# Two-layer attention and expert kernel: the second attention's query rank in three rounded products, the key rotation behind the remainders, the residual's scale behind VectorE's rotation

## What is computed

```python
kv_a = x @ w_kv_a                                # 1024 -> 256 + 64
c_kv = rmsnorm(kv_a[..., :256], kv_norm_g)
k_rope = rope(kv_a[..., 256:], cos, sin)         # the keys' rotated part, shared by the heads
kv = c_kv @ w_kv_b                               # 8 heads x (128 key + 128 value)
q = rmsnorm(x @ w_q_a, q_norm_g) @ w_q_b         # 1024 -> 384 -> 8 heads x (128 + 64)
q_rope = rope(q[..., 128:], cos, sin)
logits = q_nope . k_nope + q_rope . k_rope       # chunk-causal mask, softmax
h = (softmax(logits) @ v) @ w_o
x = layernorm(ALPHA * x + h)
# experts: router, top 2 of 32 experts in one group, silu(t @ gate) * (t @ up) @ down, weighted sum
```

## Time and profile before

| | us |
|---|---|
| median of 3 runs | 702.27 (700.65 to 704.05) |
| the profiled execution, its own time | 701.2 |
| its span in the trace | 699.4 |
| TensorE matrix products busy | 669.3 (96%) |
| VectorE, ScalarE, GpSimd busy | 321.0, 214.8, 127.9 |
| share of the chain that ended last: TensorE, transfers, SyncE's issue, VectorE | 69%, 11%, 9%, 6% |
| granted TensorE clock over the span, of full speed | 0.993 |

### The profile page before, as it was taken

The page is one execution under the profiler, slowest core; times in us unless marked ns, Lnnn a source line. Parts: engine busy times, 40 slices in busy tenths (PEclk is TensorE's granted clock), DMA queues, the critical chain, the costliest instruction groups (busy, mean ns, idle before and its releaser), DMA issues.

```text
span 699.4 us, 9824 instructions
## 1 busy us (share of the span) xinstructions
PE 669.3 (96%) x3682; PEld 383.6 (55%) x3684; DVE 321.0 (46%) x657; ACT 214.8 (31%) x420; POOL 127.9 (18%) x149
## 2 busy tenths in 40 slices
PE   9999999999999999999989798999999999999993
PEld 6969878654333433445546776866534334343551
DVE  4768755744243242232274846574424323323226
ACT  4668661531111121121146136353111211111112
POOL 0404110062010100100029570006201001010000
PEclk9999999999999999999999999999999999999998
DMA  9990049899999999999996009479999999999992
GB/s 331 364 378 3 0 176 423 343 357 391 422 419 423 421 420 422 420 421 420 415 414 255 0 8 407 196 299 369 387 421 423 420 421 421 421 420 421 421 408 97
DMA packets 42829, 237.73 MB, mean 340 GB/s; under 512 B 3920, under 2 KB 4096, under 8 KB 18720
## 3 DMA queue, kind: packets, MB, share of 16 engines
q1 hardware_dynamic: 41776, 235.36, 82.9%
q10 hardware_dynamic: 576, 1.05, 0.4%
q0 software_dynamic: 432, 0.70, 0.3%
HBM read 236.04 MB, written 1.05 MB: 339 GB/s over the span
## 4 chain that ended last, share of the span: by engine, by line
PE 69%; DMA 11%; SPq 9%; DVE 6%; ACT 2%; issue 2%; POOL 0%; DVEq 0%; POOLq 0%; ACTq 0%
PE psum L595 66%; DMA ring<-in_moe_w_up 8%; SPq L477 6%; DMA ring<-in_diff_w_qkv 3%; SPq L482 2%; PE psum L1078 1%; DVE work L442 1%; DVE ln_stats L1694 1%; SPq L462 1%; PE psum L970 1%; PE psum L918 1%; SPq L464 1%; ACT scratch L1298 0%; ACT x_res L1493 0%; PE psum L701 0%
## 5 line engine op out<-in xcount | busy, mean ns | idle before, releaser
L595 PE MATMUL psum<-ring,work 128*64 128x512 f32 (+2 forms) x1360 | 229.7, 489 | 2.1 <-POOL work L2265 1.3
L595 PEld LDWEIGHTS psum<-ring,work 128*64 128x64 f32 (+1 forms) x1360 | 99.5, 138 | 130.7 <-issue 105.6
L595 PE MATMUL psum<-ring,scratch 128*64 128x512 f32 x512 | 116.9, 598 | 0.9 <-ACT scratch L1545 0.9
L2167 DVE TENSOR_TENSOR scratch<-psum,scratch 128x256 f32<-128x256 f32 x32 | 13.6, 425 | 180.1 <-ACT scratch L1541 180.1
L2247 POOL COPY work<-work 128x512 f32 x60 | 36.7, 616 | 289.4 <-PE psum L595 285.8
L1534 ACT ACTIVATE x_T_rounded<-psum,small 128x512 fp32r<-128x512 f32 x64 | 43.6, 687 | 109.5 <-DVE scratch_rounded L2148 90.9
L1541 ACT ACTIVATE scratch<-psum 128x256 f32<-128x256 f32 x32 | 12.3, 384 | 203.0 <-PE psum L595 203.0
L595 PEld LDWEIGHTS psum<-ring,scratch 128*64 128x64 f32 x512 | 33.9, 136 | 67.9 <-issue 65.0
L595 PE MATMUL psum<-x_T_rounded,scratch_rounded 128*128 128x512 f32 x144 | 62.9, 437 | 0.9 <-issue 0.8
L595 PE MATMUL psum<-ring_rounded 128*128 128x256 f32 (+1 forms) x214 | 61.6, 309 | 0.0
L595 PE MATMUL psum<-ring_rounded,x_T_rounded 128*128 128x512 f32 x192 | 60.8, 398 | 0.0
(11 more groups left out here) (270 smaller groups left out, 829.3 us busy)
## 6 DMA issues: line engine op xcount, KB each, us to landing
ring<-in_moe_w_up SPq DMA_DIRECT2D x64, 1024.0 KB, 19.9
ring<-in_moe_w_gate SPq DMA_DIRECT2D x60, 1024.0 KB, 16.9
ring<-in_moe_w_down SPq DMA_DIRECT2D x60, 1024.0 KB, 20.0
ring<-in_diff_w_qkv SPq DMA_DIRECT2D x5, 2048.0 KB, 20.6
ring<-in_diff_w_o SPq DMA_DIRECT2D x1, 4096.0 KB, 18.7
ring<-in_moe_w_down SPq DMA_DIRECT2D x8, 512.0 KB, 23.4
ring<-in_mla_w_o SPq DMA_DIRECT2D x1, 4096.0 KB, 35.2
ring<-in_moe_w_gate SPq DMA_DIRECT2D x4, 768.0 KB, 6.1
```

What stands on the lines that cost most here:

```text
L595: return pe.matmul(dst, lhsT, rhs, start=start, stop=stop, skip_group_check=True)
L2167: dve.tensor_tensor(h_sb, psum[:, 6, FF:2 * FF], act_s, ALU.mult).then_inc(m["h_ready"], 1)
```

## The change

Four things are done.

1. The query rank is made of three rounded products. GpSimd splits `w_q_a` in three parts of 1024 columns (`qa_hi`, `qa_lo`) as soon as it is loaded and the last pair's windows are no longer read; ScalarE casts `xT` to `mx_hi` two slabs at a time, VectorE subtracts to `mx_lo`, and TensorE takes the slabs in natural order (`query_rank`). The key/value rank stays float32 (`kv_rank`).
2. VectorE rotates the keys (`rotate_keys`) after the remainders of the key/value rank and after `move(1)`, and no longer ahead of them.
3. GpSimd scales and shifts the residual of tile 1 after its query rotation and after VectorE's, and no longer first.
4. In both expert stages slabs 3 to 6 are sorted into banks 6, 7, 4 and 5 (before into 4, 5, 6 and 7; bank 6 is the one that the gate then writes), and the first windows are copied in three pieces (slabs 0 to 3, 4 and 5, 6 and 7) and not in two (0 to 5, 6 and 7); pair 0's gate waits for each piece.

```diff
@@ constants @@
-SORT_BANKS = (0, 1, 3, 4, 5, 6, 7, 2)
+SORT_BANKS = (0, 1, 3, 6, 7, 4, 5, 2)
-A_ORDER = (0, 2, 1, 3, 4, 6, 5, 7)
+X_PARTS = (3, 4, 7, 8)
+A_LO = 3
@@ build @@
-        qa = ring[1][:, 2560:5632].rearrange("p (k n) -> p k n", k=KD)
+        qa, qa_lo = (r[1][:, 2560:5632].rearrange("p (k n) -> p k n", k=KD) for r in (ring, ring_r))
+        qa_hi = work_r[:, 0:3072].rearrange("p (k n) -> p k n", k=KD)
+        mx_hi = ring_r[0][:, 9984:12032].rearrange("p (k t) -> p k t", k=KD)
+        mx_lo = work_r[:, 5632:7680].rearrange("p (k t) -> p k t", k=KD)
@@ TensorE, mla_attention @@
-                pe.wait_ge(ld_qa, 16)
...
-                def low_rank(bank, w, t, n):
-
-                    for i, k in enumerate(A_ORDER):
-                        if bank == 2:
-                            pe.wait_ge((mq["x_act"], mq["x_dve"])[i % 2], i // 2 + 1)
-                        last = mm(psum[:, bank, 0:n], xT[:, k, t * P:(t + 1) * P], w[:, k, :], i == 0, i == KD - 1)
+                def query_rank(b, which):
+
+                    for t in range(TT):
+                        tok = slice(t * P, (t + 1) * P)
+                        for k in (2 * b, 2 * b + 1):
+                            if which == 0:
+                                mm(psum[:, 2 + t, 0:QR], mx_hi[:, k, tok], qa_hi[:, k, :], k == 0, False)
+                                mm(psum[:, 2 + t, 0:QR], mx_hi[:, k, tok], qa_lo[:, k, :], False, False)
+                            else:
+                                last = mm(psum[:, 2 + t, 0:QR], mx_lo[:, k, tok], qa_hi[:, k, :], False, k == KD - 1)
+                        if which == 1 and b == 3:
+                            last.then_inc(mq["a_ps"], 1)
...
-                low_rank(2, qa, 0, QR)
-                low_rank(3, qa, 1, QR)
+                for b in range(4):
+                    pe.wait_ge(mq["w_lo"], min(b + 1, A_LO))
+                    pe.wait_ge(mq["x_act"], X_PARTS[b])
+                    query_rank(b, 0)
+                    pe.wait_ge(mq["x_dve"], X_PARTS[b])
+                    query_rank(b, 1)
@@ TensorE, moe, pair 0 @@
-                            gate_or_up(0, s, buf, range(2, 5)).then_inc(m["gate_ps"], 1)
+                            gate_or_up(0, s, buf, range(2, 4))
+                            pe.wait_ge(*m("xg0_ready", 4))
+                            gate_or_up(0, s, buf, range(4, 5)).then_inc(m["gate_ps"], 1)
                             gate_or_up(0, s, buf, range(5, 6))
-                            pe.wait_ge(*m("xg0_ready", 4))
+                            pe.wait_ge(*m("xg0_ready", 6))
@@ ScalarE, act_xt (b is 0, then 2) @@
+                    for q in (b, b + 1):
+                        act.wait_ge(*((mq["x_dve"], X_PARTS[q] - 2) if q % 2 else (mq["x_act"], X_PARTS[q] - 1)))
+                        act.copy(mx_hi[:, 2 * q:2 * q + 2, :], xT[:, 2 * q:2 * q + 2, :]).then_inc(mq["x_act"], 1)
@@ VectorE, dve_xt (b is 1, then 3) @@
+                    for q in (b - 1, b):
+                        dve.wait_ge(mq["x_act"], X_PARTS[q])
+                        dve.tensor_tensor(mx_lo[:, 2 * q:2 * q + 2, :], xT[:, 2 * q:2 * q + 2, :],
+                                          mx_hi[:, 2 * q:2 * q + 2, :], ALU.subtract).then_inc(mq["x_dve"], 1)
@@ VectorE, mla_attention: the loop over t with rotate and the copy to kr2 becomes rotate_keys() @@
+                lower_c(KVR // P, QR // P, ckv_lo, ckvT, 6, kvg)
...
                 move(1)
+                rotate_keys()
                 dve.wait_ge(mq["qr_raw"], 1)
@@ GpSimd, moe @@
-                first_windows(3, slice(0, 6))
-                first_windows(4, slice(6, KD))
+                for done, ks in ((2, slice(0, 4)), (3, slice(4, 6)), (4, slice(6, KD))):
+                    first_windows(done, ks)
@@ GpSimd, between the expert stages @@
-            scale_shift()
+            pool.wait_ge(*mo[0]("gu_ps", PAIRS))
+            pool.wait_ge(ld_qa, 16)
+            flat_hi, flat, flat_lo = (a.rearrange("p k n -> p (k n)") for a in (qa_hi, qa, qa_lo))
+            for n in range(A_LO):
+                cols = slice(n * 1024, (n + 1) * 1024)
+                chain(pool.tensor_copy(flat_hi[:, cols], flat[:, cols]))
+                pool.tensor_tensor(flat_lo[:, cols], flat[:, cols], flat_hi[:, cols], ALU.subtract).then_inc(mq["w_lo"], 1)
             for n, (w, hi, lo) in enumerate(b_parts):
...
             rotate(pool, chain, qr_rot[:, 1, :, :], qr_raw[:, 1, :, :], 1, rope_tmp2, HEADS)\
                 .then_inc(mq["qr_rot_pool"], 1)
+            pool.wait_ge(mq["rope_dve"], 1)
+            scale_shift()
             pool.wait_ge(mq["b_ps"], 4)
```

More of the change, by code:

```diff
@@ L798, in mla_attention, with kv_rank @@
                 transpose_x(2)
[L799 to L806 removed]
+                def query_rank(b, which):
[9 more added lines that the diff above has]
+                            last.then_inc(mq["a_ps"], 1)
+                def kv_rank(t):
+                    for k in range(KD):
+                        last = mm(psum[:, t, 0:KVR + ROPE], xT[:, k, t * P:(t + 1) * P], kva[:, k, :], k == 0, k == KD - 1)
                     last.then_inc(mq["a_ps"], 1)
@@ L843, in group @@
                     if g == 4:
-                        pe.wait_ge(mq["w_lo"], 5)
+                        pe.wait_ge(mq["w_lo"], A_LO + 5)
                         pe.wait_ge(mq["ct_sb"], 5)
@@ L1939, in mla_attention, with rotate_keys @@
                 normalise_c(3, 1, KVR)
-                for t in range(TT):
-                    dst = kr2[:, t, 0:ROPE].unsqueeze(1)
-                    chain(rotate(dve, chain, dst, kr_raw[:, t, :].unsqueeze(1), t, rope_tmp[:, 0:1, :], 1))
-                dve.tensor_copy(kr2[:, :, ROPE:2 * ROPE], kr2[:, :, 0:ROPE]).then_inc(mq["kr_rot"], 1)
                 lower_c(KVR // P, QR // P, ckv_lo, ckvT, 6, kvg)
+                def rotate_keys():
+                    for t in range(TT):
+                        dst = kr2[:, t, 0:ROPE].unsqueeze(1)
+                        chain(rotate(dve, chain, dst, kr_raw[:, t, :].unsqueeze(1), t, rope_tmp[:, 0:1, :], 1))
+                    dve.tensor_copy(kr2[:, :, ROPE:2 * ROPE], kr2[:, :, 0:ROPE]).then_inc(mq["kr_rot"], 1)
                 def move(g):
```

12 lines of the change are left out of this document (6 added, 6 removed).

## The result

| | before | with the change |
|---|---|---|
| median, us | 701.48 (699.81 to 704.05, 9 runs) | 698.04 (694.71 to 700.99, 9 runs) |
| ratio, 95% interval | | 0.9947 [0.9932, 0.9962] |
| the profiled execution, its own time | 701.2 | 700.99 |
| its span | 699.4 | 699.2 |
| busy: TensorE, VectorE, ScalarE, GpSimd | 669.3, 321.0, 214.8, 127.9 | 667.7, 320.1, 217.4, 139.8 |

The change takes 3.4 us off, 0.5% [0.4, 0.7]; forecast were 3.6. The profiled execution of the changed kernel is the slowest of its nine, so its span shows next to none of the gain. I therefore read it stage by stage, and later set a second execution beside it.

The account below looks back on a forecast made before the run. TensorE and the weight stream were taken to bound both expert stages, with VectorE's waits inside the second attention. Terms -1.4 + 0.3 - 5.2 + 2.7 = -3.6 us gave a median of 698.7 us, range 695.5 to 703.0.

Parts of the forecast that it names:

- the hole ahead of group 2: Second attention: TensorE waits 3.65 us for VectorE's key/value-rank remainder, then runs 3.2 us at half clock.
- What it gains, everything behind it gains: Second attention, between the expert stages: nothing streams ahead through it, so its gain passes to everything behind.
- the second expert stage no shorter from first gate to end: Listed sign that the prediction is wrong, read on the second expert stage's length; no size given.
- Part 1: First windows, both layers: gates start earlier, -0.75 and -0.65, together -1.4 us; bounds 0 and -1.6.
- no new wait: Expert stages' first gate: later slabs arrive before they are asked for, GpSimd's last at 146.50, before 147.4.
- Part 2: Query rank in rounded products: TensorE 1.3 us sooner is slack, ScalarE's norms come later; +0.3 us, bounds 0 and +1.5.
- Part 3: Remainders ahead of the keys' rotation: the 3.65 wait and half-speed stretch go; -5.2 us, bounds -3.65 and -5.25.
- Part 4: GpSimd's late residual scale puts output-weight splits under VectorE's softmax scaling of head 1; +2.7 us, bounds 0 and +3.7.
- No collision: Rival, softmax of the second attention: scaling not held or splits fall between; sum -6.3, 696.0 us; chance 0.20.
- Layer norm held: Rival: GpSimd's early query-weight splits hold VectorE's one-column layer-norm scale, +2.1, 700.8 us; chance 0.12.
- The hole only moves: Rival: key-rotation instructions and copy held by GpSimd, TensorE waits +3.4 before the keys' transposes; 702.1 us; chance 0.08.
- Clock under the rank: Rival: TensorE's clock falls under the query's rank after 0.9 us more idle time; +11.3, 710.0 us; chance 0.10.

Follow-up runs that it names:

- e6: The changed kernel with GpSimd's output-weight splits waiting for group 8 instead of 4; the edit moved nothing, so a second look at the changed kernel: 698.12 us, 0.9943.
- e3: The kernel before with only the keys' rotation moved behind the remainders and `move(1)`: 702.43 us, ratio 1.0014.
- e2: The changed kernel with the first windows, sort banks and waits as before: 698.25 us, ratio 0.9958.
- e4: e3 plus one line: GpSimd's output-weight splits also wait for VectorE's rotation of the queries: 696.58 us, ratio 0.9926.
- e5: The changed kernel with GpSimd's residual scale cut in two, the product early behind the `w_q_a` splits, the sum behind the rotation: 699.56 us, ratio 0.9964.
- e8: e4 with the new first windows and sort banks added: 696.47 us, ratio 0.9914.
- e7: The changed kernel with the query's rank as one float32 product, as before: 696.31 us, ratio 0.9921.
- e9: e5 with ScalarE taking the query rank's two norms ahead of its fifth weight cast: 696.21 us, ratio 0.9914.
- e12: The changed kernel with GpSimd's residual scale ahead of its own rotation and the query rank in float32: 695.83 us, ratio 0.9917.

## Why the prediction was right, and where it was not

The time forecast was 698.7 and 698.04 was measured, inside the range and 3.4 us under before. The main mechanism was right, the hole ahead of group 2 and its low clock; that the other terms added up is luck, as shown below. Point by point:

- **Bound.** "What it gains, everything behind it gains" held up to the second gate: *rest* is unchanged but for the clock, and the gain in *keys* arrives there (478.95 to 474.15 in `e6`). Of those 4.8 us the second expert stage gives 1.6 back (210.32 against 208.69). The prediction named "the second expert stage no shorter from first gate to end" as a sign of being wrong, and it came.
- **Part 1** (-1.4): both waits of 0.67 gone as forecast. By the timed pairs -0.8 to -1.5. The gate came early, the stream did not; "no new wait" missed the transfers of `in_moe_w_up`.
- **Part 2** (+0.3): the place was right, for the transposes stand where they stood although TensorE is through sooner, and ScalarE took up the norms 18.0 behind the end of the first expert stage (375.33; forecast 375.2, by that count 18.5). In `e6` it was 18.9, for the term took the landing of `w_q_a` from one execution, 2.9 ahead of that end, and it came 1.8 ahead. The term also left out what the new work does to GpSimd, which waits for the casts behind ScalarE's four and meets VectorE's residual in its splits. With that the part costs 1.5 to 1.8, at or just beyond the bound of +1.5.
- **Part 3** (-5.2): 30.69 to 25.34, so -5.35, the clock's share with it. The keys were ready at 396.8 (forecast 397.5) and VectorE's rotation of the queries at 399.38 (forecast 400). But the price was put on the wrong step. Moving the rotation alone gains nothing (`e3`). The prediction had the splits of `w_o` at their old 401.33 when it costed part 3, and did not ask what releases them; their wait is a count of TensorE's groups, and comes forward with TensorE.
- **Part 4** (+2.7): the collision is there, with the instruction and the place that were named. It is 1.5 us, and 1.3 in `e6` and `e2` (*head 1* 4.18, 4.01 and 3.96), not 2.7: GpSimd was 1 us ahead of the forecast, its last subtraction running since 415.68 when the scaling came at 416.35, so there was one instruction to wait for and not two. As a whole, set behind part 3, the part was costed with the wrong sign. Its wait for VectorE's rotation is what makes part 3 worth anything: 6.2 us between `e3` and `e4`. Only the scale ahead of the splits costs.
- **The rule on the ports.** The Trainium skill (SBUF — State Buffer, section "SBUF: two separate sides") has GpSimd and VectorE take a shared port pair for whole instructions. Here the trace agrees for the softmax scaling too, 2.03 against 0.54, and for instructions with two operands in SBUF, 2.50 against 0.42 in `e3`. *No collision* falls.
- **Layer norm held** falls. The one-column scale ran at its usual length inside GpSimd's subtraction, as the first line against the second shows:

```profile
359.31 0.21 DVE L1661 TENSOR_SCALAR ln_neg_mean_rstd<-ln_mean_var,ln_rstd 128x1 f32<-128x1 f32 x1
```
```profile
359.20 2.35 POOL L2388 TENSOR_TENSOR ring_rounded<-ring,work_rounded 128x1024 fp32r<-128x1024 f32 x1
```

- **The hole only moves** was given 702.1 for the full change. That did not happen, and is what part 3 alone does (702.43).
- **Clock under the rank**: it stayed at 1.00 with an idle time of 1.19 ahead. The evidence given against this rival, that waits of 1.1 had left the clock at 1.00, is weaker than it looked: at 429 the clock fell behind two such waits. In `e5` 2.29 us of idle time came with a fall to 0.86 and a loss of 1.7, a small piece of the 11.3 that this rival assumed.

The sum came out right and its terms did not. Forecast were -1.4, +0.3, -5.2 and +2.7. By the ratios of the runs, each times 701.5, it goes: keys' rotation with the wait -5.2 (`e4`), windows -0.8 (`e8` less `e4`), the scale's late place +0.5 (`e7` less `e8`), the rounded rank +1.8 (the change less `e7`), together -3.7, which is the change by its own ratio, since each step starts where the last one ended. Only the first step is clear of the noise; for the other three the stage columns are the better witness. The last two hold the collision at head 1 between them. What the rank costs more is about what the collision costs less, and that they cancel is luck.

## What to carry to other kernels

When a wait goes, look up what each engine behind it waits for. A wait on another engine's count moves forward with that engine, and can put work onto a neighbour that was clear of it; one wait the other way kept 6 us here. Price the parts of a change together: the same move was worth +1 or -5 us, and the same rounded rank nothing or some 1.7, by what stood beside it.

The smallest version, the keys' rotation moved and one wait added (`e4`), takes 5.2 us off [3.2, 7.1]; with the windows (`e8`) 6.0 [4.6, 7.6]. The measurements of `e4`, `e7`, `e8`, `e9` and `e12` do not tell these five apart.

## What the runs showed that I had not expected

- Held instructions go in turn. In `e3` VectorE's and GpSimd's alternate for five rounds, four of them shown, each of VectorE's about as long as GpSimd's (1.15 beside a cast of 1.24, 2.50 beside a subtraction of 2.44). GpSimd pays as well: its cast took 1.24 there and 1.04 in `e4`.
- A one-column scale (`TENSOR_SCALAR`, like the softmax's) runs in 0.21 beside GpSimd, while that of 128 columns is held (2.03 for two, 0.54 when free).
- The same kernel lost its clock for some 3 us in one execution and not in the next (0.57 and 1.00 from 429 to 433). `e3` and `e12` show the same loss of 1.5 to 1.7 in *rest*, the others don't.
